# A transformer pair on one core: the row halves for the retention's rotation come by transfer instead of by product

## The reference, cut to what matters

```python
def rope_rotate(x, ang):
    cos = jnp.cos(ang).astype(x.dtype)
    sin = jnp.sin(ang).astype(x.dtype)
    x1, x2 = jnp.split(x, 2, axis=-1)
    return jnp.concatenate([x1 * cos - x2 * sin, x2 * cos + x1 * sin], axis=-1)

def axial_rope(x, ang_row, ang_col):
    xr, xc = jnp.split(x, 2, axis=-1)
    return jnp.concatenate([rope_rotate(xr, ang_row), rope_rotate(xc, ang_col)], axis=-1)
```

## Time and profile before

| what | value |
|---|---|
| median of 3 runs | 2370.49 us (2370.43 to 2371.44) |
| span of the profiled execution, first to last instruction | 2365.1 us |
| PE busy | 2160.1 us (91%) |
| DVE busy | 1383.4 us (58%) |
| ACT busy | 659.3 us (28%) |
| POOL busy | 165.6 us (7%) |
| mean granted TensorE clock | 0.977 |
| chain that ended last | PE 65%, DVE 15%, DMA 13%, ACT 3% |

### The profile page before, as it was taken

The page is one execution under the profiler, slowest core; times in us unless marked ns, Lnnn a source line. Parts: engine busy times, 40 slices in busy tenths (PEclk is TensorE's granted clock), DMA queues, the critical chain, the costliest instruction groups (busy, mean ns, idle before and its releaser), DMA issues.

```text
span 2365.1 us, 40332 instructions
## 1 busy us (share of the span) xinstructions
PE 2160.1 (91%) x16524; PEld 1509.4 (64%) x16524; DVE 1383.4 (58%) x2654; ACT 659.3 (28%) x832; POOL 165.6 (7%) x221
## 2 busy tenths in 40 slices
PE   6998989988998998888998899899989999998998
PEld 5897843444454454445545555677769898876987
DVE  2566455535354443665535446866678776778866
ACT  2332120112122221211111111444443334455332
POOL 1320010000000000000000000000000000020000
PEclk9999999999999999999999999999989999999999
DMA  9888879998999999999999999444436533334651
GB/s 383 311 326 339 325 295 392 420 419 364 419 419 419 418 419 419 415 417 418 408 419 419 404 407 390 166 156 139 155 140 210 185 131 127 108 117 165 209 187 61
DMA packets 111245, 711.76 MB, mean 301 GB/s; under 512 B 12480, under 2 KB 13136, under 8 KB 36128
## 3 DMA queue, kind: packets, MB, share of 16 engines
q1 hardware_dynamic: 85904, 616.93, 66.0%
q0 software_dynamic: 25168, 92.38, 10.3%
HBM read 705.06 MB, written 4.19 MB: 300 GB/s over the span
## 4 chain that ended last, share of the span: by engine, by line
PE 65%; DVE 15%; DMA 13%; ACT 3%; issue 2%; POOL 0%; SPq 0%; DVEq 0%; ACTq 0%
PE bank L326 18%; PE bank L2373 7%; PE bank L2354 6%; PE bank L2124 4%; PE bank L2086 4%; DMA hT<-in_panels_e 3%; DMA cst<-in_panels_e 3%; DMA hid<-in_panels_e 2%; PE bank L2459 2%; DMA ring<-in_units_a 2%; PE bank L1747 2%; PE bank L2239 2%; PE bank L1581 2%; PE bank L2101 2%; PE bank L2228 1%
## 5 line engine op out<-in xcount | busy, mean ns | idle before, releaser
L326 PE MATMUL bank<-hid,scratch 128*32 128x512 f32 x1008 | 306.3, 602 | 7.0 <-DMA hT<-in_panels_e 3.8
L326 PE MATMUL bank<-hT,scratch 128*32 128x512 f32 x976 | 302.5, 608 | 10.9 <-DMA hT<-in_panels_e 9.1
L1334 ACT CAST chi<-craw 128x1024 fp32r<-128x1024 f32 x128 | 133.6, 1045 | 549.6 <-DMA craw<-in_panels_m 216.8
L3379 DVE TENSOR_TENSOR clo<-craw,chi 128x1024 fp32r<-128x1024 f32 x128 | 156.0, 1222 | 163.7 <-ACT chi L1334 162.7
L326 PE MATMUL bank<-yacc,scratch 128*32 128x512 f32 x648 | 177.4, 604 | 4.7 <-DMA diag_gtmp<-in_panels_e 4.7
L326 PE MATMUL bank<-rows,scratch 128*32 128x512 f32 x632 | 172.0, 601 | 9.9 <-DMA cst<-in_panels_e 9.7
L326 PE MATMUL bank<-cst,scratch 128*32 128x512 f32 x632 | 176.9, 609 | 2.3 <-DMA yacc<-in_panels_e 2.3
L326 PE MATMUL bank<-diag_gtmp,scratch 128*32 128x512 f32 x648 | 177.2, 600 | 2.0 <-DMA hid<-in_panels_e 1.6
L2086 PE MATMUL bank<-cT_hi,chi 128*128 128x256 f32 x384 | 112.9, 294 | 16.8 <-DVE cT_lo L3298 5.5
L326 PEld LDWEIGHTS bank<-hT,scratch 128*32 128x32 f32 x976 | 70.5, 111 | 63.5 <-issue 62.8
L2086 PE MATMUL bank<-cT_lo,chi 128*128 128x256 f32 x384 | 109.7, 286 | 0.0
(11 more groups left out here) (702 smaller groups left out, 5838.8 us busy)
## 6 DMA issues: line engine op xcount, KB each, us to landing
hid<-in_panels_e SPq DMA_DIRECT2D x96, 1024.0 KB, 13.4
hT<-in_panels_e SPq DMA_DIRECT2D x94, 1024.0 KB, 13.6
ring<-in_units_a SPq DMA_DIRECT2D x70, 1024.0 KB, 7.9
ring<-in_panels_m SPq DMA_DIRECT2D x64, 1024.0 KB, 5.1
yacc<-in_panels_e SPq DMA_DIRECT2D x48, 1024.0 KB, 12.0
diag_gtmp<-in_panels_e SPq DMA_DIRECT2D x48, 1024.0 KB, 14.1
rows<-in_panels_e SPq DMA_DIRECT2D x47, 1024.0 KB, 12.9
cst<-in_panels_e SPq DMA_DIRECT2D x47, 1024.0 KB, 13.3
```

Source lines behind the costliest of these rows:

```text
L326: m = self.pe.matmul(b[s:s + STRIP, :], lhs(k)[:, s:s + STRIP], v, start=(first and k == 0), stop=(k == KT - 1))
L1334: act.copy(chi[:, h % 2, :], context_raw(h)).then_inc(cx_hi, 1)
L3379: tt(context_lower(h), context_raw(h), chi[:, h % 2, :], ALU.subtract).then_inc(cx_lo, 1)
```

## The change

The products with `swap` go. POOL issues, for each head, two transfers from `rqk` to `ro` within SBUF: rows 64 to 127 of all four blocks to rows 0 to 63, and the reverse, 256 KB each in pieces of 1 KB. They wait for the head's four copies and, from head 1 on, for the transposes that last read `ro`. DVE's `rotated` waits for both (`halves_in`) and does its six operations with one wait among them in place of five. In head 0 it is moved from behind `lower(3)` to behind `lower(4)`. PE's `scores(0)` now takes the wait that the gate's product had. The two start semaphores become one, on which ACT, PE and DVE wait for both loads.

```diff
--- before.py
+++ after.py
@@ -634,7 +634,6 @@
         odd_turned = Pair([bank[7]] * 2, sem("odd_full"), sem("odd_free"))
         adap = Pair(bank[6:8], sem("ada_full"), sem("ada_free"))
         rowp = Pair(bank[0:2], sem("row_full"), sem("row_free"))
-        ident_in = sem("ident_in")
         lower_in = sem("lower_in")
         first_in = [sem(f"first_in{n}") for n in range(FRONT_SLOTS)]
         unit_used = sem("unit_used")
@@ -690,6 +689,7 @@
         sum_free = sem("sum_free")
         rot = Pair(bank[2:4], sem("rot_full"), sem("rot_free"))
         rot_up = sem("rot_up")
+        halves_in = sem("halves_in")
         hi_ready = sem("hi_ready")
         lo_ready = sem("lo_ready")
         unit_done = sem("unit_done")
@@ -962,7 +962,7 @@
                         unit(at(src, i * 2 + (2 + j // 2)), j % 2)
 
             sp.dma_start(params[:, :, :], a["params"].rearrange("(t p) n -> p t n", p=P)).then_inc(params_in, 16)
-            sp.dma_start(cst[:, 0:P], a["consts"][:, 0:P]).then_inc(ident_in, 16)
+            sp.dma_start(cst[:, 0:P], a["consts"][:, 0:P]).then_inc(params_in, 16)
             order = first_units()
             late = len(order) - 2 * LATE
             for n, (_, _, _, words) in enumerate(order[:late]):
@@ -1137,6 +1137,14 @@
                     .then_inc(cx_back, 16)
                 pool.dma_start(rv[:, 2:4, :], kv[i][:, 2 * SEQ:].rearrange("p (a n) -> p a n", a=2)).then_inc(cx_back, 16)
 
+            def swapped_halves(i):
+                pool.wait_ge(qk_free, 4 * i + 4)
+                if i:
+                    pool.wait_ge(rot.full, 2 * i)
+                v = ro.rearrange("p t (b n) -> p (t b) n", n=SEQ)
+                for to, src in ((0, 64), (64, 0)):
+                    pool.dma_start(v[to:to + 64, :, :], rqk[src:src + 64, :, 0:SEQ]).then_inc(halves_in, 16)
+
             for n in range(4):
                 pool.wait_ge(rows_used, n + 1)
                 for j, name in enumerate(("ln_g_2", "ln_b_2")):
@@ -1144,6 +1152,7 @@
                 if n == 0:
                     for i in range(RET_HEADS):
                         context_back(i)
+                        swapped_halves(i)
                 if n == 1:
                     loads = Count()
 
@@ -1175,7 +1184,7 @@
             to_dve = Post(act, from_act)
             to_tensor = Post(act, act_to_pe)
 
-            act.wait_ge(params_in, 16)
+            act.wait_ge(params_in, 32)
             to_tensor.send(act.activation(params[:, 0, :], params[:, 0, :], ACT.Silu))
 
             def root(n, first=0):
@@ -1555,8 +1564,7 @@
             from_a = Post(pe, act_to_pe)
             per_gemm = lambda fills, panels: {G.c: fills, G.others: fills - panels, G.panels: panels}
 
-            pe.wait_ge(ident_in, 16)
-            pe.wait_ge(params_in, 16)
+            pe.wait_ge(params_in, 32)
             pe.wait_ge(filled, ONES_FILLED)
             from_a.get()
             b = S.open()
@@ -2243,16 +2251,8 @@
                     elif half:
                         m.then_inc(vg_full, 1)
 
-            def swapped():
-                for n in range(2):
-                    b = S.open()
-                    for j in range(2):
-                        m = pe.matmul(b[:, j * SEQ:(j + 1) * SEQ], swap, rqk[:, 2 * n + j, 0:SEQ], start=True, stop=True)
-                    S.close(m)
-
             def scores(i):
-                if i:
-                    from_dve.get()
+                from_dve.get()
                 for n in range(4):
                     if n == XT:
                         pe.wait_ge(cx_back, 32 * (i + 1))
@@ -2300,11 +2300,7 @@
                 for which in range(2):
                     for half in range(2):
                         columns(i, which, half, n + 2 * which + half)
-                        if i == 0 and which == half == 0:
-                            pe.wait_ge(qk_free, 4)
-                            swapped()
                         if i == 0 and half and not which:
-                            from_dve.get()
                             spread_gate(1, settle=False)
 
             from_dve.get()
@@ -2325,9 +2321,6 @@
                 turn_rows()
                 if more:
                     queries_keys(i + 1, 1, n + 1)
-                    pe.wait_ge(qk_free, 4 * i + 8)
-                    R.read()
-                    swapped()
                 first = n + 2 if more else n
                 sums(i, 0, first)
                 sums(i, 1, first + 1)
@@ -2759,7 +2752,7 @@
             ada_product(0)
             for j in range(1, 4):
                 ada_before(j)
-            dve.wait_ge(ident_in, 16)
+            dve.wait_ge(params_in, 32)
             ada_turn(3)
             G.settle()
             scales(0, 0, {0: (parcol[:, 0:8], None)}, (0,))
@@ -3598,16 +3591,15 @@
 
             def rotated(i):
                 dve.wait_ge(qk_free, 4 * i + 4)
+                dve.wait_ge(halves_in, 32 * (i + 1))
+                other = [ro[:, n, :].rearrange("p (a b) -> p a b", a=2) for n in range(2)]
+                own = [rqk[:, 2 * n:2 * n + 2, 0:SEQ] for n in range(2)]
                 for n in range(2):
-                    b = S.take()
-                    S.done(tt(ro[:, n, :].rearrange("p (a b) -> p a b", a=2), b[:, :].rearrange("p (a b) -> p a b", a=2),
-                              rope[:, :, 1, :], ALU.mult))
-                    S.settle()
-                    step(tt(rqk[:, 2 * n:2 * n + 2, 0:SEQ], rqk[:, 2 * n:2 * n + 2, 0:SEQ], rope[:, :, 0, :], ALU.mult))
-                    m = tt(rqk[:, 2 * n:2 * n + 2, 0:SEQ], rqk[:, 2 * n:2 * n + 2, 0:SEQ],
-                           ro[:, n, :].rearrange("p (a b) -> p a b", a=2), ALU.add)
-                    if n == 0:
-                        step(m)
+                    tt(other[n], other[n], rope[:, :, 1, :], ALU.mult)
+                    m = tt(own[n], own[n], rope[:, :, 0, :], ALU.mult)
+                step(m)
+                for n in range(2):
+                    m = tt(own[n], own[n], other[n], ALU.add)
                 to_tensor.send(m)
 
             def distances():
@@ -3683,11 +3675,11 @@
             context(POINTS * TURNS + 1)
             queries_keys(0, 1, 1)
             lower(3)
-            rotated(0)
             gate_cols(1, 2, (1,))
             diagonals(gmul[:, 0, :])
             distances()
             lower(4)
+            rotated(0)
             spread(0)
             decays()
             lower(5)
```

## The result

The changed kernel takes 2399.38 us (median of 4 runs, 2391.57 to 2407.39), the kernel before in the same comparison 2370.97 us (4 runs, 2370.43 to 2372.15): a ratio of 1.0122, 95% interval 1.0103 to 1.0141. It is 28.4 us slower. The sign of the forecast was right; its size was 8.5 us, and the time lies above the range (2370 to 2387 us).

What follows compares the result with a forecast made beforehand. The prediction took DVE's chain before unit n+4, not PE, to bound the retention. Head 0 +1.8, heads 1 to 3 +1.0 and the clock +5.7 made +8.5 us, so 2379.0 us, range 2370 to 2387.

Steps and rivals of the forecast that it cites:

- What bounds the kernel: Retention, heads 1 to 3: DVE's chain, not PE, sets unit n+4; removing PE's swap, 2.15 us a head, gains nothing.
- rival B: Retention: PE is the bound after all, so its removed 8.0 us are gained, giving 2362.5 us; chance 0.06.
- DVE's part: Rotation, heads 1 to 3: six operations take 3.77 us instead of 4.23, saving 0.46 us a head.
- The start: Program start: ACT waits some 0.2 us more for the identity, hidden by PE's 2.85 us wait for a load.
- The transfers, heads 1 to 3: DVE's wait before rotation: second half lands at 1565.9, 0.75 to 0.8 us new waiting, net +0.3 us a head, +1 us.
- Head 0: Retention's first head: halves land late behind POOL's 1.75 MB, delaying unit 5 by +1.8 us, bounds +0.5 and +3.6.
- T: Head 0: time the halves land, taken as 1523.2, bounds 1521.9 and 1525; PE starts unit 5 at T + 10.14.
- The clock: PE's gaps of 2.9 us, 4.8 in head 0, bring half clock: 1.9 us an event, three events, +5.7 us.
- The sum: Whole kernel: +1.8 + 1.0 + 5.7 = +8.5 us on a span of 2365.1, median 2379.0 us.
- Rival C: Transfers share DMA engines badly with the weight load: 6 us from issue, +2.6 us a head, 2390 us; chance 0.12.
- The rule weighed against the row: 256 KB flight: skill's rule gives 2.6 us, saving 1.4 in heads 1 to 3; `context_back` row, used, gives 3.1.

Runs made afterwards that it cites:

- e3: Changed kernel, same transfers but reading constants into a spare place, DVE not waiting, exchange left out; retention 270.2 us, runs 2373.51 us, ratio 1.0008.
- e6: Kernel before, swap products kept, with the rotation of heads 1 to 3 moved to its place in e5; retention 269.2 us, runs 2371.42 us, ratio 1.0001.
- e5: Changed kernel, rotation moved behind lower(n+5) and the distances, head 0 behind lower(5); retention 257.1 us, runs 2358.50 us, ratio 0.9937.
- e8: Changed kernel, transfers issued by SP ahead of the colliding weight load instead of by POOL; retention 277.2 us, single run 2369.87 us.
- e1: Kernel before with the two start semaphores made one, nothing else; retention 270.3 us, runs 2370.72 us, ratio 0.9989.
- e10: Changed kernel, POOL still issuing, SP's weight load in heads 1 to 3 held back until the halves land; retention 284.3 us, single run 2381.53 us.
- e2: Changed kernel with the two start semaphores kept apart; retention 300.3 us, runs 2397.29 us, ratio 1.0113.
- e4: Changed kernel, rotation moved behind lower(n+7), head 0 behind lower(5); retention 265.9 us, runs 2365.89 us, ratio 0.9974.

## Why the prediction was right in its sign and wrong in its size

- **What bounds the kernel: right.** The removed products were hidden. e3 has neither products nor wait, and its retention is as long as before. Their size was taken too low: from the last query/key product to the second product of the projection it is 2.86 us with the swap (e6) and 0.35 us without (e5), 2.5 us a head and not 2.15, and 9.3 us in all where the forecast and rival B had 8.0. That is PE's idle time and costs the sum nothing; it makes the gaps 0.3 us longer than the forecast's 2.9 us, as e8's 3.15 us show.
- **DVE's part: right.** The rotation takes 1586.49 - 1582.67 = 3.82 us, forecast 3.77.
- **The start: right.** Nothing, by e1.
- **The transfers, heads 1 to 3: the step that failed.** I put the second landing 3.7 us after its own issue, 3.1 for the flight and 0.6 for the load, hence +0.3 us a head. The flight was taken from a row with nothing before it, and the load in flight was priced as half of a fair share. Measured: 7.2 to 7.6 us for the second half; the first is issued at 1574.71, the rotation starts at 1582.67, so 7.96 us from issue to use where the forecast had 4.4; DVE waits 4.5 to 4.7 us, and with the 0.46 us saved it is +4.0 to +4.2 us a head, 12.2 us for +1.0. e10 splits it: with the load out of the way the first half takes 3.12 us, as the row said, and the second 3.75, so the first half costs the second 0.6 us, which the forecast did not have, and the load costs 3.5 us in head 1, which it had at 0.6. The load was issued 0.6 to 0.8 us ahead of the halves, and its packets went first; only then came a share. e10 shows that this load is the cause. The order of issues at that moment was to be had from the trace of before: the end of the query/key unit is what releases SP's load as well as DVE's copy, and SP has no copy between.
- **Head 0: the same step, smaller.** I took T = 1523.2 on the axis of before, with 1525 as upper bound. Measured: the halves land 11.2 and 14.8 us after their issues, the second at 1532.2, which on that axis (4.3 us earlier) is 1527.9; a DVE wait of 8.24 us where I had said about 3, and unit 5 at 1542.33, there 1538.0 against 1531.58: +6.4 us for +1.8. My upper bound was +3.6. Half a megabyte read behind a queue of 1.75 MB also meets the weight loads; I gave that 1.25 us and "a little".
- **The clock: right in kind, close in size.** It fell in all four heads: the 24 products behind the gaps took 8.10, 7.35, 7.45 and 8.53 us instead of 5.86, so 2.2 + 1.5 + 1.6 + 2.7 = 8.0 us for +5.7. Two of three gaps at 2.9 us became three of three at 7; e8, with 3.15 to 3.17 us, lost it in all three as well, so taking all four would have been nearer; e3, with 2.45 us, lost it in two of three.
- **The sum**: 6.4 + 12.2 + 8.0 = 26.6 us of 26.7. What lies between this and the 28.4 of the medians is ahead of the retention, within the spread of the start.
- **Rival C had the mechanism** (a bad share with the weight load) and still too small a price: 6 us from issue, +2.6 a head, head 0 at its upper bound. I gave it 0.12 because the one row at hand was a transfer on free engines, and a load of 1 MB beside it seemed a matter of tenths. The upper bound of the landing, 1.6 us later, came from no row with two queues at work; the earlier trace rows is one, 9.8 us for 512 KB, and I had used it for head 0 only.
- **The rule weighed against the row.** By the Trainium skill (DMA: Bandwidth & Descriptors, Anatomy of one DMA), with its fixed 2.0 us and the bytes at 436 GB/s, 256 KB take an estimated 2.6 us, which made a saving in heads 1 to 3. The measured times are 3.1 and 3.7 us for the two halves with the load out of the way (e10) and 6.6 and 7.2 us behind it, so the measurement decides against it here. The Trainium skill (DMA: Bandwidth & Descriptors, Issuing engines are not separate DMA queues) says that transfers of all issuers run on the same engines and interleave. The rows of 1578 to 1582 us agree; those of 1574 to 1578 us, with not one packet of the later queue, say that interleaving does not start at once (3.4 to 3.7 us after the issue, against 1.2 us with no load in the way, e10).

What stays open: why head 0's landing differs by 2.5 us between e2 and the changed kernel, and whether the halves' packets are late because their descriptors are made late or because the engines have the load's packets queued. e10 shows that without the load they are not late, which speaks for the queue.

## What to carry to other kernels

A transfer that replaces work on an engine is priced from its issue to its use, behind whatever another queue issues at the same event: ask what the same semaphore releases on SP, and take the row of a transfer that met such a load, not of one alone. If the work it replaces was hidden, the transfer gains nothing where the work stood; it gains (here 12.1 us in the retention against the same move without the transfer; 0.63% of the run against before) once the consumer is moved behind other work that covers the flight, and then its speed does not matter. And put such a consumer ahead of the next engine's deadline, not as late as possible: two units later (e4) gave 8.8 of those microseconds back.

## What was not expected of the hardware

- 256 KB within SBUF, issued by POOL 0.8 us after a 1 MB load of SP, landed after 6.3 to 7.6 us (heads 1 to 3; in head 0, behind 1.75 MB of POOL's own, 11.2 and 14.8 us) and moved its first packet 3.4 to 3.7 us after the issue; with the load held back, 3.1 and 3.7 us, first packet after 1.2 us; issued by SP ahead of the load, 3.3 and 3.9 us.
- The same size from HBM under the same load, heads 1 to 3: 5.4 to 7.1 us. The way within SBUF is no shorter than the way from HBM.
- From 1578 to 1582 us the two queues together moved 244 GB/s at a DMA share of 0.97, where the page of the changed kernel has slices of 419 GB/s with loads of 1 MB. The low rate is that of the halves, not of the sharing: alone they moved 221 GB/s at a share of 0.99 (e10, 1571.3 to 1573.3 us) and 234 GB/s at 0.99 (e8, 1561.5 to 1563.5 us).
- POOL begins an issue 0.28 to 0.53 us after the instruction that releases it, SP 0.02 us.
- Products that compute nothing, put into gaps of 3 to 7 us, shortened the retention by 3.1 and 4.0 us, since the clock stayed at 2.4 GHz; the 96 products behind each gap took 1.4 and 2.0 us less.
